# Queries of the samples first, states by heads, and two DMA queues for the cache pages

## The reference

```
proj = rms_norm(x) @ w_in                       # 1024 -> 4608 columns, 520 rows
rq, rk, rv, rg, dq, dk, dv = split(proj)
rq, rk = rope(rq), rope(rk)                      # 4 heads of 128
ro, state = retention(rq, rk, rv, state0)        # values 4 x 256; state 128 x 256 per head
ro = head_group_norm(ro) * silu(rg)
dq, dk = rope(rms_norm(dq)), rope(rms_norm(dk))  # 4 heads x 2 x 64
# a sample also reads 32 pages of 128 keys and values of its past, by page_table
do = (softmax(q1 k1) - lam * softmax(q2 k2)) @ v
mix = concat(ro, rms_norm(do) * gain) @ w_out    # 1536 -> 1024
```

## Time and profile before

| | us |
|---|---|
| median of 3 runs | 2041.03 (2038.61 to 2042.01) |
| the profiled execution | 2045.41 |
| its span, first to last instruction | 2043.6 |
| busy: PE, DVE, ACT, POOL | 1882.8, 909.9, 568.6, 636.0 |
| mean granted TensorE clock | 0.952 of full |

### The profile page before, as it was taken

The page is one execution under the profiler, slowest core; times in us unless marked ns, Lnnn a source line. Parts: engine busy times, 40 slices in busy tenths (PEclk is TensorE's granted clock), DMA queues, the critical chain, the costliest instruction groups (busy, mean ns, idle before and its releaser), DMA issues.

```text
span 2043.6 us, 35465 instructions
## 1 busy us (share of the span) xinstructions
PE 1882.8 (92%) x14237; PEld 1683.9 (82%) x14237; DVE 909.9 (45%) x1155; ACT 568.6 (28%) x915; POOL 636.0 (31%) x510
## 2 busy tenths in 40 slices
PE   4967888899998799999999999979999999999998
PEld 4855555555554599999999899879999999999997
DVE  2577676665552544332333423393323443323331
ACT  4422333322231232221222232303313333212221
POOL 1388554777740013300431100023304224102400
PEclk8988898999996799999999999979999999999999
DMA  6258686899997223332323322202322232332221
GB/s 206 92 165 270 232 258 207 315 335 356 337 320 243 94 83 94 99 92 90 92 93 93 95 63 82 67 10 74 101 86 92 89 98 83 104 91 86 92 93 63
DMA packets 218268, 287.95 MB, mean 141 GB/s; under 512 B 12977, under 2 KB 149762, under 8 KB 217858
## 3 DMA queue, kind: packets, MB, share of 16 engines
q1 hardware_dynamic: 215306, 281.95, 41.8%
q10 hardware_dynamic: 2208, 2.75, 0.4%
q0 software_dynamic: 624, 1.44, 0.4%
HBM read 274.89 MB, written 11.21 MB: 140 GB/s over the span
## 4 chain that ended last, share of the span: by engine, by line
PE 81%; DVE 8%; DMA 3%; ACT 3%; SPq 2%; issue 2%; POOL 1%; ACTq 0%; DVEq 0%
PE ps L1639 18%; PE ps L1641 18%; PE ps L1640 18%; PE ps L1449 6%; PE ps L1451 5%; PE ps L1450 5%; PE ps L1495 4%; DMA vbuf<-in_cache_v 2%; DVE Sc L1138 1%; PE ps L1540 1%; POOL kbuf L633 1%; PE ps L1706 1%; PE ps L1422 1%; PE ps L1527 1%; PE ps L1519 1%
## 5 line engine op out<-in xcount | busy, mean ns | idle before, releaser
L488 DVE TENSOR_TENSOR w_lo<-raw,w_hi 128x1024 fp32r<-128x1024 f32 x238 | 334.7, 1414 | 498.2 <-ACT w_hi L481 497.1
L1639 PE MATMUL ps<-xg_hi,w_hi 128*128 128x260 f32 x1408 | 398.6, 283 | 0.5 <-DVE sTs L1409 0.5
L1641 PE MATMUL ps<-xg_hi,w_lo 128*128 128x260 f32 x1408 | 398.4, 283 | 0.0
L1640 PE MATMUL ps<-xg_lo,w_hi 128*128 128x260 f32 x1408 | 397.3, 282 | 0.0
L633 POOL TENSOR_TENSOR kbuf<-kbuf,Qb 128x512 f32<-128x512 f32 x256 | 344.4, 1373 | 141.0 <-DMA kbuf<-in_cache_k 140.9
L481 ACT ACTIVATE w_hi<-raw 128x1024 fp32r<-128x1024 f32 x248 | 259.1, 1054 | 460.9 <-PE ps L1641 413.0
L1449 PE MATMUL ps<-w_hi,xg_hi 128*128 128x256 f32 (+1 forms) x1200 | 352.4, 294 | 21.8 <-DVE w_lo L488 9.4
L1450 PE MATMUL ps<-w_lo,xg_hi 128*128 128x256 f32 (+1 forms) x1200 | 344.6, 287 | 0.0
L1451 PE MATMUL ps<-w_hi,xg_lo 128*128 128x256 f32 (+1 forms) x1200 | 344.2, 287 | 0.0
L1641 PE MATMUL ps<-h_hi,w_lo 128*128 128x260 f32 x1024 | 289.3, 283 | 0.0
L1639 PE MATMUL ps<-h_hi,w_hi 128*128 128x260 f32 x1024 | 289.1, 282 | 0.0
(11 more groups left out here) (274 smaller groups left out, 2543.0 us busy)
## 6 DMA issues: line engine op xcount, KB each, us to landing
kbuf<-in_cache_k SPq DMA_DIRECT2D x256, 256.0 KB, 4.5
vbuf<-in_cache_v SPq DMA_DIRECT2D x256, 256.0 KB, 4.9
raw<-in_w_ffn_up SPq DMA_DIRECT2D x64, 512.0 KB, 3.8
raw<-in_w_ffn_down SPq DMA_DIRECT2D x64, 512.0 KB, 3.5
raw<-in_w_in_odd SPq DMA_DIRECT2D x48, 512.0 KB, 3.8
raw<-in_w_in_even SPq DMA_DIRECT2D x36, 512.0 KB, 5.5
raw<-in_w_out_odd SPq DMA_DIRECT2D x24, 512.0 KB, 3.6
raw<-in_w_out_even SPq DMA_DIRECT2D x12, 512.0 KB, 3.6
```

The source lines that it names most:

```text
L488: dve.tensor_tensor(w_lo[:, c.slot], raw[:, c.slot % 2], w_hi[:, c.slot].bitcast(F32), ALU.subtract).then_inc(lo_made, 1)
L1639: pe.matmul(out, wh, xh, start=kk == 0, stop=False, skip_group_check=True)
L1640: pe.matmul(out, wh, xl, start=False, stop=False, skip_group_check=True)
L1641: mm_ = pe.matmul(out, wl, xh, start=False, stop=kk == KC * groups - 1, skip_group_check=True)
```

## The change

- **Order of tiles.** A list `TILES` of 90: the samples' tiles of macros 0 and 1 first, then the prompt tiles of 0 and 1, and from macro 2 on the samples' tile first. The samples' queries and keys have a norm and rotation of their own (`ropeS`, on 8 rows of 512); `rope` does the four prompt tiles alone and copies nothing. So `qb` comes after the second prompt tile of macro 0.
- **Steps of the past** begin at tile 4 of the list, four for every three tiles; `LAG` is 22; 39 of 153 steps lie behind the last tile, two in each slot. The softmax of a sample comes two steps later than it did. The attention units come one every 1.5 tiles from tile 30.
- **States by heads.** `sx` at tile 56; from tile 60 on, head by head and 8 tiles apart, four `sU` (PE makes the outer products of two samples, DVE adds them to a 256 KB state tile) and one `sO` (8 matmuls with the queries). SP loads four tiles a head, ScalarE stores them. `OUT` serves these too.
- **Mixed rows.** `so1`, `so2`, `soT` and the 12 `mix` steps are steps of the list, behind the last tile beside the remaining pages. The rows lie over the spent input (`ma`) and over `rv`, `sg` (`mb`); the next stages have their rows in other places (`xb`, `h_hi`, `g_hi`).
- **Queues.** ScalarE issues the value pages (`values_in` at each `V` step of its own list), SP the key pages, weights and states. SP reloads the first three of eight blocks of x after the last key page, the rest after the last value page.
- **Prologue.** The sample rows and chunks 0 and 1 come before x; chunks 2 and 3 land in a buffer of their own (`early`). DVE makes all low parts; POOL only multiplies key pages.
- **Start of the projection.** The first macro runs half by half: 260 prompt tokens first, and the half with the samples after their rows are done.

```diff
+def _tiles():
+    seq = [(0, NT), (1, NT)]
+    for m in range(N_IN):
+        seq += [(m, NT)] * (m > 1) + [(m, t) for t in range(NT)]
+    return seq
...
-LAG = SPS + 4
+LAG = SPS + 6
+FIRST_STEP = 4
...
+    for i in range(len(UNITS)):
+        j = AT[6, NT] + 3 * i // 2
+        middle[j].append(("dA", i))
+        first[j + 1].append(("dE", i))
+        first[j + 2].insert(0, ("dT", i))
+        late[j + 2].append(("dB", i))
...
+        j = AT[12, NT] + 8 * h
+        first[j - 1].append(("sL", h))
+        first[j - 1].append(("sM", h))
+        for p in range(NS // 2):
+            first[j + p].append(("sU", h, p))
+        first[j + NS // 2].append(("sO", h))
+    first[NTILE].append(("so1",))
+    first[NTILE + 1].append(("so2",))
+    first[NTILE + 2].append(("soT",))
+    for b in range(12):
+        first[NTILE + b // 2 + 2 * (b > 5)].append(("mix", b))
...
+        n = max(0, (j - FIRST_STEP + 1) * 4 // 3) - step if j < NTILE else 2
...
+        def values_in(act, v, n):
+            if v < NG:
+                wait(act, v_used, v + n - V_SLOTS)
+                for i, pg in enumerate(pages(v, n, mybir.EngineType.Activation)):
+                    page(act, vbuf[(v + i) % V_SLOTS][:, :], cache_v, pg, v_loaded[(v + i) % V_SLOTS])
...
+                elif kind == "sU":
+                    h, p = step[1:]
+                    pe.wait_ge(k_masked, h + 1)
+                    pe.wait_ge(nat_read, AT[10 + 2 * h, NT] + 1)
+                    wait(pe, out_read, OUT_FILL[step])
+                    for n in range(2):
+                        last = pe.matmul(ps[:, OUT, DVR * n:DVR * n + DVR], kmask[:, 2 * p + n, :], srv[:, DVR * h:DVR * h + DVR],
+                                         start=True, stop=True, skip_group_check=True)
+                    last.then_inc(out_ready, 1)
...
+            act.wait_ge(xg_lo_made, KD)
+            act.wait_ge(xs_made, 1)
+            act.wait_ge(x_saved, 16)
+            for v in range(0, V_SLOTS, QUAD):
+                values_in(act, v, QUAD)
+            act.wait_ge(rstd_sample, 1)
...
+            def prompt_first(c0, groups, high, low):
+                pe.wait_ge(nat_read, NTILE)
+                pe.wait_ge(o_copied, NS - 1)
+                pe.wait_ge(mix_lo, 12)
+                for hf in range(2):
+                    if hf:
+                        pe.wait_ge(out_read, len(OUT_FILL))
+                        pe.wait_ge(mix_lo, 13)
```

More of the change, by code:

```diff
@@ L123, in plan @@
[L123 to L132, removed]
+    slots = NTILE + 40
+    first, middle, late = ([[] for _ in range(slots)] for _ in range(3))
@@ new lines, in plan @@
+    first[AT[1, NT]].append(("ropeS", 0))
+    for i in range(2):
+        first[AT[0, 1]].append(("qb", i))
+    first[AT[3, NT]].append(("ropeS", 1))
+    first[AT[3, 1]].append(("snew",))
+    for m in ROPED:
+        first[read_of(m)].append(("rope" if m < 4 else "rot", m))
+        for hh in range(2):
+            first[read_of(m) + 5 + hh].append(("turn", m, hh))
+    for i in range(len(UNITS)):
[4 more added lines that the diff above has]
+        late[j + 2].append(("dB", i))
@@ L133, in plan @@
+    j = AT[6, NT] + 3 * len(UNITS) // 2 + 2
+    for q in range(NT):
+        first[j + q].append(("dnorm", q))
+    first[AT[11, 1]].append(("sx",))
     for h in range(H):
-        line = [(11 + 2 * h, t) for t in range(NT + 1)]
-        after[12 + 2 * h, 0].append(("rS", h))
+        j = AT[11 + 2 * h, NT]
         for n in range(NT):
[L137 to L142, removed]
@@ L143, in plan @@
-    step = 0
[L144 to L157, removed]
+            first[j + 6 + n].append(("rC", h, n))
@@ L158, in plan @@
+    for b in range(12):
+        first[NTILE + b // 2 + 2 * (b > 5)].append(("mix", b))
+    after = [[] for _ in range(slots)]
+    step = 0
+    for j in range(slots):
+        n = max(0, (j - FIRST_STEP + 1) * 4 // 3) - step if j < NTILE else 2
+        now = []
+        for _ in range(n):
             if step < STEPS:
-                after[N_IN, NT] += kv_step(step)
+                now.append(kv_step(step))
                 step += 1
[L161 to L164, removed]
+                if step == NS * SPS + 7:
+                    now[-1] = now[-1] + [("fz",)]
+        after[j] = first[j] + (now[0] if now else []) + middle[j] + [s for step_ in now[1:] for s in step_] + late[j]
@@ L175, in constants @@
+MIX = [s[1] for s in ORDER if s[0] == "mix"]
 def constants():
@@ L1608, in _ @@
-            pe.wait_ge(f_squared, 1)
-            pe.matmul(ps[:, TURN, 128:160], ones[:, :], fr, start=True, stop=True, skip_group_check=True).then_inc(f_ss, 1)
-            pe.wait_ge(so_done, 1)
-            pe.wait_ge(out_read, len(OUT_FILL))
-            for b in range(8):
-                last = turn(ps[:, OUT, NS * b:NS * b + NS], sro[:, P * b:P * b + P], NS)
-            last.then_inc(mix_ready, 1)
-            pe.wait_ge(mix_lo, 14)
-            def wide(name, per, src_hi, src_lo, ready, counts, e=None, first=1):
+            for j, now in enumerate(AFTER):
+                if j < NTILE:
+                    m, t = TILES[j]
+                    if j == 0:
+                        pe.wait_ge(xs_made, 1)
+                    if j == AT[0, 0]:
+                        pe.wait_ge(xg_lo_made, KD)
+                    if t == NT:
+                        pe.wait_ge(lo_made, 2 * m + 2)
+                    wait(pe, nat_read, j - 1)
+                    natural([Chunk(0, 0, 0, 2 * m + g) for g in range(2)], t, NAT[j % 2], xg_hi, xg_lo, NT - 1)
+                for step in now:
+                    pe_step(step)
@@ L1620, in wide @@
+            def wide(name, per, high, low, ready, counts, e=None, first=1, begin=None):
                 c0, groups, macros = PHASES[name]
@@ L1624, in step @@
                         s = mm % 2
+                        if begin is not None and isinstance(i, int) and i == 0 and mm == 0:
+                            begin(c0, groups, high, low)
+                            continue
                         wait(pe, acc_read, 2 * per * i + (BLOCK0[name] + 2 * mm - 2))
```

670 lines of the change are left out of this document (371 added, 299 removed).

## The result

| | us |
|---|---|
| before, median of 4 runs | 2041.52 (2038.61 to 2045.26) |
| after, median of 4 runs | 2072.38 (2069.12 to 2073.69) |
| ratio, 95% interval | 1.0149 (1.013 to 1.0167) |
| predicted | 1998 (1938 to 2038) |

The account below looks back on a forecast made before the run. It saw one page stream, DMA-bound only from 398.6 to 597 us, with DMA idle at head and tail. Terms 54 + 145 + 180 + 209 + 70 + 3 = 661 to the projection, against 704.0, gave 1998 us (1938 to 2038).

Parts of the forecast that it names:

- The head: From the start to the first key score: keys start at 54 us (50 to 60) instead of 111.
- A: Tiles 4 to 30, with 72 key and 28 value pages: 145 us (99 to 179), from a DVE demand of 136.
- B: Tiles 30 to 54, with 16 attention units, 64 key and 64 value pages: 180 us (162 to 227).
- the end: From the last value matmul to the output projection: 3 us (2 to 8), where 33 us lay before.
- C: Tiles 54 to 90, with 46 steps and 184 pages: 209 us, 5.8 a tile (186 to 238).
- D: Behind the tiles, 28 key and 72 value pages, 22 MB still to move: 70 us (64 to 79).
- TensorE's demand: In C: tiles 102, values 24, retention 24, states 29, the rest 5, together 184 us, beside 186 of DMA.
- surcharge: In C: two engines at the same demand, coupled in order and through the OUT bank, take 209 us.
- the 1 us that I had set as the sign: Forecast wrong if PE's states and retention wait for the OUT bank longer than 1 us a tile.
- The first claim: The question is how much idle DMA time at the head (to 111 us) and tail (from 597) is recovered.
- the head start is given back: Rival: keys start 57 us earlier, but A at 179 and B at 205 eat it; 720 against 704; chance 0.06.
- The rival of ScalarE's bursts: Rival: 2.4 us issue bursts for 39 quads of B and C fall on the path, 94 us, 2092; chance 0.11.

Follow-up runs that it names:

- run 3: The changed kernel without the samples' state work (no state loads, outer products, query products or stores): 2045.96 us, ratio 1.0000.
- run 12: The changed kernel with one of the three products of each projection tile left out from tile 54 on: 2053.08 us, ratio 1.0054.
- run 9: The changed kernel with value pages by SyncE, two steps a tile from tile 54, first head's states by ScalarE, values requested one step sooner: 2021.28 us, ratio 0.9902.
- run 10: The changed kernel with value pages issued by SyncE and each value quad requested one step sooner: 2048.90 us, ratio 1.0035.
- run 11: The kernel before the change, with each value quad requested one step sooner: 2038.05 us, ratio 0.9977.
- run 4: The changed kernel with two steps a tile from tile 54 on, leaving 13 steps instead of 39 behind the last tile: 2057.56 us, ratio 1.0063.
- Run 15: As run 9, but the steps of key and value pages begin at tile 16 instead of tile 4: 2021.43 us, ratio 0.9883.
- run 5: The changed kernel with value pages issued by SyncE and two steps a tile from tile 54 on: 2042.87 us, ratio 1.0011.
- run 13: As run 9, but all value pages behind the first eight are issued by ScalarE: 2050.73 us, ratio 1.0031.

## Why the prediction was wrong

**What held.** The head (54 predicted, 55.9 measured), A (145 us long, 149.5), B (180, 182), the end (3, 1.6), the unchanged rest (1340, 1339). The projection came 71 us later than the forecast 661: 44 of them are C, 20 are D. B held with its mechanism: the mixing instructions of the 16 units came 11.4 us apart. A's number was luck in part. Its sum rests on a DVE demand of 136 us; DVE was busy 108.6 (POOL 98.6 of the 99 forecast), and late key pages held GpSimd for 50 us there.

**The step that failed: C, "Two engines at the same demand ... do not both reach it: 5.8 us a tile, 209".** It measured 253, 7.0 a tile, above even the upper end of 238. By size, the mis-sized term is TensorE's demand: 184 and a surcharge of 25 were forecast, about 225 and 28.5 us of waits for value pages were measured. The surcharge had the right size for the wrong reason.

- *TensorE's demand, put at 184.* From one matmul's start to the next's, the projection tiles took 119 us and not 102, retention and states 64 and not 53, and what the forecast called the rest 18 and not 5 (some 12 of them idle, before transpositions and broadcasts). With the value steps, and without the 28.5 us that TensorE waited for value pages, that is about 225 us. Of the 17 us of the tiles, 9 are the granted clock: six of the 35 tiles ran wholly or partly at half the full clock. The forecast took all tiles at the 2.84 us of a stretch with the full clock. Here is the start of a tile's 24 matmuls and of the instruction behind them, first at the granted clock 1.00 (2.94 us), then at 0.50 (5.26 us):

```profile
384.23 0.37 PE L1545 MATMUL ps<-w_hi,xg_hi 128*128 128x256 f32 x1
...
387.17 0.60 PE L1517 MATMUL ps<-cst,pq 128*128 128x128 f32 x4
...
426.38 0.56 PE L1545 MATMUL ps<-w_hi,xg_hi 128*128 128x256 f32 x1
...
431.64 0.86 PE L1693 MATMUL ps<-rv,scm 128*128 128x256 f32 x2
```

Runs 3 and 12 show that TensorE's work counts: without some 32 us of states, or 40 of products, the kernel is 30 and 19 us faster.

- *The coupling, taken as a small surcharge.* It was priced as two engines that miss their demand a little, with the upper end from a stretch of the old list. What decides is when a slot is asked for again, and that stands at a step of the list. Thinner steps ask later: 7.8 us for 4.8. Moving the request by one step gave 17 and 15 us (runs 9, 10), and 5 in the old list, between 0 and 10 by its interval (run 11). The one `OUT` bank, which the forecast also blamed, was a small part at most: all that TensorE was idle in C for other things than value pages is 21 us, 0.6 a tile, under the 1 us that I had set as the sign. I had read the old rate off without asking what kept the queue fed at it.

**D, "70".** It measured 90, above its upper end of 79: 25 MB at 279 GB/s, where 22 MB in 70 us (314 GB/s) were forecast. There TensorE has no tiles to do and waits for each quad; the chain at the end:

```profile
715.94 0.31 ACTq L544
716.28 0.04 ACTq L548
716.41 0.34 ACTq L548
716.90 0.34 ACTq L548
717.40 4.10 DMA vbuf<-in_cache_v
721.50 0.04 issue
721.54 1.69 PE ps L1591 x4
```

A quad that is used up frees its slots, ScalarE asks for four pages, the first matmul waits for them: with two quads of buffers the DMA is not filled (279 GB/s). Leaving less work for D paid: 57 us of D for 33 of C in run 4.

**The first claim, "how much of the idle DMA time at the head and the tail the new order recovers".** Run 15 shows it empty, in the list of run 9: the head start of 50 us can be given up for nothing. (In the change as it stood, with 1.33 steps a tile, this wasn't tried.) A has idle DMA but not idle engines; a step there costs DVE and GpSimd about 3 us of a tile's time, and behind the tiles it costs 2. The rival "the head start is given back" had this in the wrong place: it let A and B grow, and they took the time forecast. The time went in C. The old list did two steps a tile in 6.6 us; the new one, with 1.33 steps a tile and the states beside them, took 7.0. The tiles grew no shorter for the steps that were moved out of them.

**The rival of ScalarE's bursts** (chance 0.11, 2092) had the sign. As the change stood, the issues cost 8 us, not told from nothing, 11 once the steps were denser (run 5 against 4), and 26 once the requests were in time (run 13 against 9). That late requests had hidden them is a guess: the old list asks as late by steps, and lost 32 us by the same edit, 19 of them behind the head. Nor did the loss come the way the rival had it: before the first product of a tile TensorE was idle 0.0 us in C, so it didn't wait for the evacuation of a projection bank. I argued the issues away with ScalarE's idle share. That share says nothing of an in-order engine that stands at a semaphore: the wait alone costs 9 us in a fast list. The Trainium skill (DMA: Bandwidth & Descriptors, "Issuing engines are not separate DMA queues") says that DMAs of several engines run on the same 16 DMA engines, and that several issuers save only issue time. The runs agree that nothing is gained; here the issue time moved to ScalarE was itself the largest part, 12 of 26 us, of a loss.

**Settled and open.** From 1.0149 to 0.9902 of before, 50 us, the runs show: denser steps in C 18, value pages off ScalarE 8 to 11 on the way, requests in time 17; the first states are left, 2 to 5, with intervals that overlap. Open is whether the last 5 us of two queues with big transfers are real, and whether they come from key pages that land late or from the lower granted clock: both were seen, and neither was tested by itself. Open is also why TensorE's clock was granted less often in C than in the old full stretch (0.92 against 0.98).

## What to carry to other kernels

Idle bandwidth is only worth something where the engines that use the bytes are idle too; price a step of the stream in each stretch before moving it, not the bytes. When a list is made thinner or denser, look at every request that is tied to "n steps later": the distance in time changes with it, and a ring of two groups shows it at once. Issue loads from an engine that does nothing else, or count its wait, its issues and all that stands behind them.

## What of the hardware I had not expected

- ScalarE's wait and issues, 62 times with 4 transfers of 4 bytes each, made the kernel 21 us slower, though ScalarE was busy only 0.31 of the time from 205 to 387 us and 0.25 from 440 to 590 (0.55 in the 53 us between tile 54 and 440).
- The same 256 KB pages from two issuing engines landed up to 13.7 us after the issue, from one up to 8.8, at a lower total rate (319 against 359 GB/s from 440 to 590 us) and a lower granted clock (0.85 against 0.95).
- The granted clock in C was 0.92 and in D 0.85, against 0.98 in the old full stretch, and run 9 had 1.00 from 440 to 500. So matmuls took longer in just the stretches where TensorE waited more, and taking work away (run 12: ten slow tiles for six) gave back less than its own time.
